# Idle TensorE slots around norms, gates and weight splits of a three-block forward pass: constants, order and split points changed

## The reference

```python
# first block: dilated + stick-breaking attention, then
h = h + (gate_a * ya + gate_b * yb) @ w_out
n = rms_norm(h, ln_x_g); m = rms_norm(mem, ln_mem_g)
h = h + memory_cross_attn(n, m, w_xq, w_xkv, w_xo)
n = rms_norm(h, ln_ffn_g)
h = h + conv_gated_mlp(n, w_up, conv_w, conv_b, w_down)   # width-3 causal convolution, silu(gate) * value
# second block, layers 0 and 1
h = h + 0.5 * rms_norm(swiglu(rms_norm(h, g0), w13, w2), g1)
m = gmlp_mixer(...)   # layer 0: u, v = split(gelu(z)); v is normalised over its 2048 columns, then mixed
m = rwkv7_mixer(...)  # layer 1: a recurrence over the tokens
h = h + rms_norm(m, g3); ... second swiglu ...
gate = sigmoid(rms_norm(h, g6) @ ple_w_gate)
h = h + rms_norm(gate * (p @ ple_w_proj), g7)
```

## Time and profile before

| what | value |
|---|---|
| median of 3 runs | 3356.26 us (3353.33 to 3357.06) |
| the profiled execution | 3353.66 us, its span 3351.8 us |
| PE busy | 3246.0 us, 97% of the span |
| DVE, ACT busy | 1783.8 us, 1216.4 us |
| mean granted clock of PE | 0.988 of full speed |

### The profile page before, as it was taken

One profiled execution on the slowest core, in us unless ns is written; L12 is line 12 of the kernel. 1 busy time (PEld: TensorE's weight loads), 2 busy tenths in 40 slices (PEclk: granted clock), 3 DMA queues, 4 the chain that ended last, 5 costly groups with the idle time before them and its releaser, 6 DMA issues.

```text
span 3351.8 us, 46666 instructions
## 1 busy us (share of the span) xinstructions
PE 3246.0 (97%) x20408; PEld 2648.9 (79%) x20408; DVE 1783.8 (53%) x2112; ACT 1216.4 (36%) x1532; POOL 97.2 (3%) x100
## 2 busy tenths in 40 slices
PE   8999998999999999999999999999899999999997
PEld 6877786888878888988788887888767787788886
DVE  5446664777354434454644347443376664754437
ACT  3346643323132222342332235222235564332224
POOL 2000000000000001000100011000000000100001
PEclk9999999999999999999999999999999999999998
DMA  5211231222322223222222222222212100122231
GB/s 191 79 51 51 76 114 63 88 95 82 103 97 89 100 87 115 101 77 99 85 98 97 87 99 83 101 96 83 98 70 72 50 4 16 70 101 101 86 103 63
DMA packets 45979, 286.47 MB, mean 85 GB/s; under 512 B 5952, under 2 KB 6224, under 8 KB 19920
## 3 DMA queue, kind: packets, MB, share of 16 engines
q1 hardware_dynamic: 44240, 280.34, 23.8%
q0 software_dynamic: 1536, 3.15, 0.4%
HBM read 278.22 MB, written 2.10 MB: 84 GB/s over the span
## 4 chain that ended last, share of the span: by engine, by line
PE 78%; DVE 5%; ACT 2%; issue 1%; DVEq 0%; ACTq 0%
PE ps L508 68%; PE ps L3153 3%; DVE wl L331 1%; PE ps L3191 1%; ACT wh L315 1%; PE ps L974 1%; PE ps L1204 1%; PE ps L1205 0%; PE ps L1206 0%; DVE xl L2627 0%; PE ps L2457 0%; PE ps L833 0%; DVE xl L1064 0%; DVE tmp L2635 0%; PE ps L3198 0%
## 5 line engine op out<-in xcount | busy, mean ns | idle before, releaser
L508 PE MATMUL ps<-xh,wh 128*128 128x512 f32 (+1 forms) x2464 | 966.6, 393 | 23.7 <-DVE xl L1064 10.6
L508 PE MATMUL ps<-xl,wh 128*128 128x512 f32 (+1 forms) x2464 | 945.7, 390 | 0.2
L508 PE MATMUL ps<-xh,wl 128*128 128x512 f32 (+1 forms) x2464 | 920.1, 391 | 0.0
L331 DVE TENSOR_TENSOR wl<-raw,wh 128x2048 fp32r<-128x2048 f32 (+1 forms) x284 | 591.3, 2082 | 454.4 <-ACT wh L315 454.1
L315 ACT CAST wh<-raw 128x2048 fp32r<-128x2048 f32 (+2 forms) x281 | 487.6, 1735 | 292.9 <-PE ps L508 285.7
L508 PEld LDWEIGHTS ps<-xh,wh 128*128 128x128 f32 (+1 forms) x2464 | 462.5, 188 | 133.4 <-issue 28.4
L508 PEld LDWEIGHTS ps<-xl,wh 128*128 128x128 f32 (+1 forms) x2464 | 462.2, 188 | 100.8 <-DVE xl L1064 2.3
L508 PEld LDWEIGHTS ps<-xh,wl 128*128 128x128 f32 (+1 forms) x2464 | 461.9, 188 | 98.8 <-issue 1.0
L508 PE MATMUL ps<-hid_h,wh 128*128 128x512 f32 x880 | 343.6, 390 | 2.8 <-DVE wl L331 2.8
L508 PE MATMUL ps<-hid_l,wh 128*128 128x512 f32 x880 | 343.1, 390 | 0.0
L508 PE MATMUL ps<-hid_h,wl 128*128 128x512 f32 x880 | 342.9, 390 | 0.0
(11 more groups left out here) (421 smaller groups left out, 3995.6 us busy)
## 6 DMA issues: line engine op xcount, KB each, us to landing
raw<-in_up SPq DMA_DIRECT2D x88, 1024.0 KB, 4.7
raw<-in_down SPq DMA_DIRECT2D x64, 704.0 KB, 4.1
raw<-in_up_c SPq DMA_DIRECT2D x22, 1024.0 KB, 4.7
raw<-in_down_c SPq DMA_DIRECT2D x16, 704.0 KB, 4.1
raw<-in_gates SPq DMA_DIRECT2D x8, 1024.0 KB, 4.7
raw<-in_gv SPq DMA_DIRECT2D x8, 1024.0 KB, 4.8
raw<-in_gu SPq DMA_DIRECT2D x8, 1024.0 KB, 4.7
raw<-in_gout SPq DMA_DIRECT2D x8, 1024.0 KB, 4.7
```

The costliest lines, as they stand in the source:

```text
L331: nc.vector.tensor_tensor(wl[:, slot, 0:w], raw[:, slot, 0:w], wh[:, slot, 0:w].bitcast(F32), ALU.subtract).then_inc(lo_ready, 1)
L508: last = nc.tensor.matmul(out, stationary, moving, start=(fresh and q == 0), stop=(t == kt - 1 and half == per - 1 and q == 2), skip_group ...
```

## The change

In words, in the order of the program:

- **Memory norm.** With `scale_first`, DVE does `scale_dve` of `mem_norm` ahead of `split_lo` of the chunk for the next product, no longer behind it.
- **Norm before the convolution's up product.** PE gets 5 constants as soon as its last product is done (`lead`), 3 in place of 2 between the sum and the spread, 4 in place of 3 behind the spread.
- **Convolution's last tile.** ACT and DVE split the second chunk of `down_c` inside the last unit of `up_c`: ACT ahead of that unit's silu, DVE between the convolution and the product with the gate. `second_ahead` takes that split out of `down_c`.
- **gMLP.** Root and scale of v move from unit 1 to unit 2 of `gu`, behind the split of the chunk for unit 3.
- **Gates, both layers.** In the last pair the second tile is scaled, opened (sigmoid) and multiplied in two halves of 256 tokens. DVE adds the first tile's squares between the two steps, where it used to add them ahead of the second tile's scaling.
- **First norm of layer 1.** 6 constants in front of the sum.
- **Front of the recurrence (`to_hn`).** 3 constants ahead of the first spread (none before), 6 behind it, 2 ahead of each of the last six of the eight sums of squares, 3 ahead of the second spread, 7 in place of 5 behind it.
- **Final norm.** 5 constants ahead of the sum, 3 ahead of the spread.

```diff
@@ -333,7 +333,7 @@
                tokens=EVERY, last_rows=P, norms=None, sums=False, between={}, parted=False, behind={}, gives=None,
-               split_ahead=False, joint=False, paired=False, third=False):
+               split_ahead=False, second_ahead=False, joint=False, paired=False, third=False):
@@ -390,6 +390,8 @@
                 n += 1
+            if second_ahead and (unit, half) == (0, 0):
+                return None
             if unit % lots or n >= len(order) or (paired and unit == 3) or (late and not paired and unit == 1):
@@ -464,10 +466,10 @@
                     norms.squares_dve(dve)
-                    if paired:
+                    if paired or norms.scale_first:
                         norms.scale_dve(dve)
                     split_lo(dve, n, n % 2, order[n][2])
-                    if not paired:
+                    if not paired and not norms.scale_first:
                         norms.scale_dve(dve)
@@ -806,7 +808,7 @@
-        def sum_up(self, pe):
+        def sum_up(self, pe, between=0):
             if self.quarters and self.by == "before":
@@ -815,6 +817,8 @@
                 for t in range(KD):
+                    if t > 1:
+                        keep_busy(pe, between)
                     self.sum_tile(pe, t)
@@ -836,10 +840,10 @@
-        def pe(self, pe, idle):
+        def pe(self, pe, idle, between):
             if not self.quarters:
                 pe.wait_ge(psum_read.sem, self.evicted)
-            self.sum_up(pe)
+            self.sum_up(pe, between)
             if self.quarters:
@@ -934,8 +938,8 @@
-        def __init__(self, *passes, idle=(2, 3)):
-            self.idle = idle
+        def __init__(self, *passes, idle=(2, 3), lead=0, between=0):
+            self.idle, self.lead, self.between = idle, lead, between
             self.passes = [Pass(0, by="tensor" if n else "before", **p) for n, p in enumerate(passes)]
@@ -943,8 +947,13 @@
         def pe(self, pe):
-            for p in self.passes:
-                p.pe(pe, self.idle[0])
+            if self.lead:
+                pe.wait_ge(psum_read.sem, self.passes[0].evicted - 1)
+                keep_busy(pe, self.lead)
+            for n, p in enumerate(self.passes):
+                if n:
+                    keep_busy(pe, self.idle[2])
+                p.pe(pe, self.idle[0], self.between)
             keep_busy(pe, self.idle[1])
@@ -980,8 +989,9 @@
         def __init__(self, gain, post=None, source=None, split=x_split, tokens=EVERY, keep=None, summed_before=False,
-                     total=None, here=None, stat=0, arrived=None):
-            self.arrived = arrived
+                     total=None, here=None, stat=0, arrived=None, lead=0, scale_first=False):
+            self.arrived, self.scale_first = arrived, scale_first
+            self.lead = lead
             self.here = here
@@ -1020,6 +1030,9 @@
             if self.post:
+                if self.lead:
+                    pe.wait_ge(psum_read.sem, self.evicted - 1)
+                    keep_busy(pe, self.lead)
                 self.post.sum_up(pe)
@@ -1115,7 +1128,7 @@
     def split_norm(gain, source=None, split=x_split, tokens=EVERY):
-        return Norms(dict(source=h if source is None else source, gain=gain, split=split, tokens=tokens))
+        return Norms(dict(source=h if source is None else source, gain=gain, split=split, tokens=tokens), idle=(3, 4), lead=5)
@@ -1930,7 +1943,8 @@
     MEMORY = slice(0, MEM)
-    mem_norm = Deferred(VEC["ln_mem"], source=mem, split=mem_split, tokens=MEMORY, keep=mem_rs, total=mem_rs, here=mem_here, stat=12)
+    mem_norm = Deferred(VEC["ln_mem"], source=mem, split=mem_split, tokens=MEMORY, keep=mem_rs, total=mem_rs, here=mem_here, stat=12,
+                        scale_first=True)
     linear("w_out", KD, 256, x_split, norms=Made(lambda t: t // 2 * 2 + 2), between={1: (mem_norm.split_act, mem_norm.split_dve)},
@@ -2164,6 +2178,8 @@
                                                conv[:, side, back:T], ALU.mult, ALU.add).then_inc(dve_steps.sem, 1)
+        if k == KF - 1:
+            split_lo(dve, second_down, second_down % 2, order[second_down][2])
         dve.wait_ge(dve_steps.sem, dve_steps.after(k, 6))
@@ -2171,14 +2187,19 @@
+    second_down = first["down_c"] + 1
...
+    def split_second_down(act):
+        split_hi(act, second_down, 16 * (second_down // 2 + 1), second_down % 2, order[second_down][2])
...
     def conv_act(act, k, products, u):
...
     linear("up_c", KD, 256, x_split, act_part=conv_act, dve_part=conv_dve, steps=(2, 8),
-           norms=split_norm(VEC["ln_ffn"]))
-    linear("down_c", HALF, P, hid_split, halves=True, norms=Made(lambda t: 8 * t + 8), **summing(h, 1, onto=True))
+           norms=split_norm(VEC["ln_ffn"]), between={KF - 1: (split_second_down, None)})
+    linear("down_c", HALF, P, hid_split, halves=True, second_ahead=True, norms=Made(lambda t: 8 * t + 8), **summing(h, 1, onto=True))
@@ -2192,8 +2213,8 @@
-    def pre(layer, n, after):
-        return Deferred(gain(layer, n), post=after)
+    def pre(layer, n, after, lead=0):
+        return Deferred(gain(layer, n), post=after, lead=lead)
@@ -2215,6 +2236,9 @@
         return {5: (split_act, split_dve)}
...
+    PARTS = (slice(0, T // 2), slice(T // 2, T))
+    g_part, g_part_open = roles("gate_parts", "gate_parts_open")
@@ -2233,12 +2257,17 @@
         def last(self, act, k, products, u, wait_product):
-            for m in range(2):
-                act.wait_ge(dve_steps.sem, dve_steps.after(k, 3 * m + 1))
-                self.sigmoid(act, k, u, m)
-                if m == 0:
-                    act.wait_ge(dve_steps.sem, dve_steps.after(k, 2))
-                    self.square(act, k, u, m)
+            act.wait_ge(dve_steps.sem, dve_steps.after(k, 1))
+            self.sigmoid(act, k, u, 0)
+            act.wait_ge(dve_steps.sem, dve_steps.after(k, 2))
+            self.square(act, k, u, 0)
+            for n, part in enumerate(PARTS):
+                act.wait_ge(g_part.sem, g_part.base + n + 1)
+                x = tmp[:, 2 * u + 1, part]
+                opened = nc.scalar.activation(x, x, ACT.Sigmoid)
+                opened.then_inc(g_part_open.sem, 1)
+            act.wait_ge(g_part_open.sem, g_part_open.base + 2)
+            act.sem_inc(act_steps.sem, 1)
             nc.scalar.activation(spare[:, 0:1], spare[:, 1:2], ACT.Sqrt).then_inc(act_steps.sem, 1)
@@ -2280,18 +2309,23 @@
             dve.wait_ge(dve_steps.sem, dve_steps.before(k, 2, 6))
-            for m in range(2):
-                wait_product(dve, m)
-                self.scaled(dve, k, products, u, m)
-                if m:
-                    dve.wait_ge(dve_steps.sem, dve_steps.after(k, 4))
-                    dve.sem_inc(psum_read.sem, 1)
-                self.gated(dve, k, u, m, 2 * m + 1)
-                if m == 0:
-                    self.add(dve, k, u, 0, 2, 2)
-            dve.wait_ge(dve_steps.sem, dve_steps.after(k, 5))
-            nc.vector.tensor_tensor(tmp[:, 2 * u + 1, :], proj[:, 2 * k + 1, :], proj[:, 2 * k + 1, :],
-                                    ALU.mult).then_inc(dve_steps.sem, 1)
+            wait_product(dve, 0)
+            self.scaled(dve, k, products, u, 0)
+            self.gated(dve, k, u, 0, 1)
+            wait_product(dve, 1)
+            for part in PARTS:
+                nc.vector.tensor_tensor(tmp[:, 2 * u + 1, part], products[1][:, part], rs[:, part], ALU.mult).then_inc(g_part.sem, 1)
+            self.add(dve, k, u, 0, 2, 2)
+            dve.wait_ge(g_part.sem, g_part.base + 2)
+            dve.sem_inc(dve_steps.sem, 1)
+            dve.sem_inc(psum_read.sem, 1)
+            dst = proj[:, 2 * k + 1, :]
+            for n, part in enumerate(PARTS):
+                dve.wait_ge(g_part_open.sem, g_part_open.base + n + 1)
+                nc.vector.tensor_tensor(dst[:, part], tmp[:, 2 * u + 1, part], dst[:, part], ALU.mult).then_inc(g_part.sem, 1)
+            dve.wait_ge(g_part.sem, g_part.base + 4)
+            dve.sem_inc(dve_steps.sem, 1)
+            nc.vector.tensor_tensor(tmp[:, 2 * u + 1, :], dst, dst, ALU.mult).then_inc(dve_steps.sem, 1)
             last_squares[0] = tmp[:, 2 * u + 1, :], dve_steps
@@ -2357,6 +2391,8 @@
         norm.beside(lots)
+        g_part.stage(4, 1)
+        g_part_open.stage(2, 1)
         linear(f"ple_gate{layer}", KD, 256, x_split, norms=norm, act_part=GateAct(), dve_part=GateDve(norm, lots), steps=(4, 6),
@@ -2512,7 +2548,7 @@
-        linear("gu", KD, 256, x_split, act_part=u_act, dve_part=u_dve, steps=(1, 1), between={0: (statistics_act, statistics_dve), 1: (root_act, scale_dve)},
+        linear("gu", KD, 256, x_split, act_part=u_act, dve_part=u_dve, steps=(1, 1), between={0: (statistics_act, statistics_dve), 2: (root_act, scale_dve)},
                third=True,
@@ -2524,7 +2560,7 @@
     embed(0, Beside(gain(0, 6), post(ybuf, 0, 5)))
-    feed_forward(1, 0, pre(1, 0, post(proj, 0, 7, sums_p)))
+    feed_forward(1, 0, pre(1, 0, post(proj, 0, 7, sums_p), lead=6))
```

(5 more changed lines are left out.)

## The result

The changed kernel takes 3333.83 us (median, 3332.24 to 3336.96) where the kernel before takes 3354.80 beside it (3352.83 to 3357.06): ratio 0.9938, 95% interval 0.9926 to 0.9950. Against my base of 3356.26 another 1.5 is the level of before itself, whose median over the five later comparisons lies between 3353.8 and 3356.9.

A forecast was written before the change was run, and what follows sets the result against it. PE, busy 97% of the span, was taken as the bound, so only its idle and half-clock time could be saved. Eight terms summed to 15.1 us, off 3356.26 giving 3341, range 3335 to 3348.

The forecast's parts named there:

- Memory norm: Scale ahead of the weight split removes nearly all of PE's 2.33 us wait: 2.2 us saved.
- gMLP: Earlier split removes PE's whole wait for unit 3's low weights in gu: 2.4 us saved; unit 4 charged nothing.
- Convolution's last tile: Early splits remove PE's wait before down_c's second chunk, 2.8 us, and the half clock behind it, 1.7: together 4.5.
- Gates: Halved gated tile lets layer 0's sum start earlier: 1.3 us saved; layer 1's gate 0, with 0.3 either way.
- layer 1's first norm: Constants keep the clock up: 1.75 us at the norm and 0.6 in the next product's ramp, together 2.3.
- Up product: Norm before the convolution's up product: constants keep the clock up, DVE's idle falls from 2.10 to 1.20: 0.9 us saved.
- rival 2: New PE wait behind the up product's first unit, possibly with half clock: 1.7 us back, 3342.7; chance 0.16.
- Recurrence's front: Constants keep the clock up at both norm spreads, 0.48 + 0.68, less 0.3 for constants between sums: 0.8 us saved.
- End: Final norm: constants keep the clock up, DVE's idle falls from 1.88 to 1.20: 0.7 us saved.
- rival 4: Timed executions may have half clock behind the 2.33 and 2.44 waits: up to 2 x 1.7 more saved, 3338; chance 0.12.
- Rivals 3, 5, 6 and 7: Clock falls at norms anyway: 3345.7, 0.12; half-clock constants: 3364, 0.03; waits reappear downstream: 3349, 0.05; no effect: 3356, 0.02.
- rival 8: All slow time is PE's: the recurrence's front gives back 10.2 us instead of 0.8, 3332; chance 0.02.

The follow-up runs named there:

- e8: Changed kernel with the convolution's edit put back and six constants filling the wait before down_c's second chunk: 3337.87 us.
- e12: Changed kernel with the gates put back to whole tiles, no halves: 3335.46 us.
- e3: Kernel before plus only the four edits of order (memory norm, convolution, gMLP, gates), no added constants: 3338.23 us, ratio 0.9951 to before.
- e18: Changed kernel with constants in three remaining waits, plus 50 tiny unread matmuls in PE's first wait: 3331.20 us, ratio 0.9929 to before.
- e16: Changed kernel with constants in three remaining waits (cross attention, behind the recurrence's norm, ahead of rk): 3336.57 us.
- e17: Changed kernel with 18 tiny matmuls in PE's first wait, results unread: 3336.94 us.
- e10: Changed kernel with the memory norm's order put back and five constants filling PE's wait ahead of its spread: 3338.57 us.
- e11: Changed kernel with gMLP's root and scale put back behind unit 1 and five constants filling the wait at unit 3: 3340.85 us.
- e6: Changed kernel with only gMLP's root and scale put back behind unit 1: 3340.75 us.

## Why the prediction was wrong

The direction and the sum's places held; two terms were too small, and one was missing. By its steps:

- **Memory norm**, 2.2: the order did what I said, and its wait is worth 2.5. What failed is that I read "no half clock behind it" off one trace. With a fall in 2 of 5 traces at 1.7, the term is about 2.5 + 0.7 = 3.2.
- **gMLP**, 2.4: the wait is worth 2.7, and a fall in 3 of 5 adds 1.0: 3.7. Unit 4's weights were not late.
- **Convolution's last tile**, 4.5: the wait 3.1 (filled, e8) rather than 2.8, the clock 4/5 of 1.6: 4.4. Right in size; that the fall comes every time was read off one trace here too.
- **Gates** and layer 1's first norm, 1.3 + 2.3: 3.8 against one trace, 3.7 against the mean of three. The halves alone are 1.2 (e12). Layer 1's halves, which I costed at 0, are worth 0.3.
- **Up product**, 0.9: 1.6 against the first trace and 0.9 against the other two of before, 1.2 on the mean; rival 2's wait of 1.21 is in it. e3 has the 1.6 without a constant, since the clock did not fall there: so behind this wait, too, it does not fall every time, and no run shows what the constants alone are worth.
- **Recurrence's front**, 0.8: 0.7 and 0.8. **End**, 0.7: 0.9 without layer 1's gate.

These make 3.2 + 3.7 + 4.4 + 3.7 + 1.2 + 0.8 + 1.0 = 18.0 where the sum said 15.1. They are estimates from one trace per run, with falls counted over five traces each. By them rival 4 was the right mechanism, and mis-weighted: 0.12 for what two of five and three of five traces show; its mean of 1.7 belonged in the sum. The failed step is the reading of the memory norm and of `gu`: 2.2 + 2.4 = 4.6 where the traces make it 6.9, and where putting the one or the other back cost + 5.2 and + 6.9 in the timed executions. Rivals 3, 5, 6 and 7 did not come. Nor did rival 8: the front gave 0.7, as its rows said, and not the 10 that it priced.

The other step that failed isn't in the sum: it charged nothing to code that no edit touches. The remaining 3 of the 21 are in such stretches, mostly the recurrence, where PE can run out of instructions at every 256th record and each edit of PE's stream moves where that is. In the two first traces this accounts for the recurrence: before is longer by 3.1 at its four places (0.9 + 0.5 + 1.0 + 0.7, more than the gaps' own 1.9), the changed kernel by 1.3 at its own two, and the difference is 1.8 of the column's 2.0. That the gaps move with the stream is shown by seventeen programs, in which PE's records lie in ten different ways. That moving them can move the time is borne out by e18 against e16 (5.4) and e17 (+3.1), each a median of five; most of the first and a part of the second is falls of the clock beside the gaps, by the traces.

What stays open: how much of the 3 is the blocks' in the timed executions. The length of a gap at the same record differs between executions (0.57 and 0.94 at the first), and with it the time that the packet took (0.93 and 1.37; at the third place gaps of 0.60 and 1.03 with packets of 1.25 and 1.51). The four sum to 1.9, 2.8, and 0.9 in e3, whose recurrence is 2.8 shorter with the blocks unmoved: 1.2 at the gaps, and 1.6 for the fall at 2832, which e3 has not. So the recurrence's gain in the changed kernel may be part blocks, part chance. Nor is it settled why e10, e11 and e6 lose more than their place and its share of falls (3 to 5 us) in every execution, or why a gap costs more than its length. In e6, e11, e16 and e18 the clock fell once more at 2620 to 2628 (1.6 by the shifts), in none of the other sixteen traces; what brings it on there was not tried.

## What to carry to other kernels

Behind the waits of 2.3 to 2.8 us here the clock fell in some executions and not in others: price such a wait at its length plus a share of 1.7, from several traces, not at what the one trace shows. Removing it gained here; filling it with constants narrowed the range at two places of three and lowered no median. Where small matmuls run at full rate, look for "issue" gaps, count PE's records to them, and compare them with the times of the instruction packets. See whether some instructions in an idle slot elsewhere move them to a better place, take the measured time and not the gaps for the judge, and measure again after every edit of PE's stream. Put one part back in the faster kernel rather than alone into the slower one, if the faster one is the steadier.
